# Retention inside the input product of the second mixer, head by head, with the sample states in 32 pieces

## The chip, the cores and the metric

The kernel runs on one core of a Trainium2 chip. The metric is the device time of one execution in microseconds (us); a kernel's time is the median of its runs. Of the core's engines, PE (TensorE) multiplies and transposes, DVE (VectorE) and ACT (ScalarE) do elementwise work, POOL (GpSimd) and SP (SyncE) mostly start DMA transfers. Each engine works through its own instructions in the written order, and semaphores hold one engine until another has got far enough.

## The reference

One step of a decoder with two layers for a prompt of 256 tokens and 8 samples of 4 tokens each (T = 288 token columns in all), everything in float32. A layer is a mixer, a cross-attention to 256 memory tokens and a convolutional FFN, each between norms. Layer 1's mixer is the retention that is changed here:

```python
z = h @ w_in_odd[o]                       # 1024 x 6144
q, k, v, g = jnp.split(z, [nq, 2 * nq, 2 * nq + nv], axis=-1)   # 4 heads: q, k 256 wide, v, g 512 wide
q = rope(q...) * (RET_DK ** -0.5); k = rope(k...)
r, s_new = retention(q, k, v, s_prev, log_g)   # prompt: two chunks of 128; samples: one chunk of 4 each
r = (r - mean(r)) * rsqrt(var(r) + EPS)        # per head and token
out = (silu(g) * r) @ w_out_odd[o]             # 2048 x 1024

# one chunk of retention, per head h, gamma = exp(log_g[h]):
scores = (q @ k.T) * dmat
o = scores @ v + (q @ s_prev) * q_decay
s_new = gamma ** L * s_prev + (k * k_decay).T @ v
```

The samples bring `state_retention`, 8 x 4 matrices of 256 x 512, and return as many: 16.8 MB in and 16.8 MB out. The prompt starts from zero and returns four such matrices.

## The kernel before, in words

**A weight product.** `Gemm` describes a product; all of them share one pipeline. A chunk is 1024 rows of 256 weight columns (1 MB). SP loads it into one of four slots of `raw` (L286). ACT rounds it to `wh` (L324), DVE takes the rest `wl = raw - wh` (L327), both in two buffers. PE then runs two tiles of 128 output columns per chunk, each of 24 matmuls over T columns: `wh*hh + wh*hl + wl*hh` for 8 row blocks (L392, helper `products`). A buffer of `wh` comes free when PE is through with both tiles of its chunk (`w_used`), and a slot of `raw` when `wl` is made (`lo_ready`).

**The second mixer** (`pe_odd`, `act_odd`, `dve_odd`, `pool_retention`) has two stages. First the input product, 24 chunks and 48 tiles in the order of the weight's columns: all q and k (DVE turns them by the rope, L876 to L880), all v, all g. Behind some of its chunks PE turns values and keys into token rows. Then the retention of all heads in 8 units, `UNITS` = (head, chunk of the prompt). Unit n also handles sample n, for all four heads: 8 matmuls of 512 columns read its old states (L1194, four heads at once in the four column groups of the array, into one bank), 8 matmuls give its new key-value products (L1207, two banks in turn), and after each of these DVE updates a quarter state in place (L946, `update`). PE's order in a unit is written out by hand: scores, old states, products, chunk state (L1229), output (L1236, L1241), products, transposes of the normed rows (L556).

**The states** stand in the four slots of `raw`, two samples at a time, 1 MB each half. SP starts their loads (`load_states`, L303) after the weight chunks of the product; from the third sample on a load waits until POOL's store of the slot (L584) has landed. The weights of the output product `w_out_odd` come behind them in SP's queue (L284 waits for the last two stores).

**The output product** (L392 again) starts when DVE has written the low part of the gated samples (L1005).

Of the kernel before, what the change touches and what calls it, by code (L numbers as in the profile page):

```python
# [15 lines left out]
F32 = mybir.dt.float32  # L16
# [5 lines left out]
P = 128  # L22
# [41 lines left out]
def build(nc, a, outs):  # L64
# [31 lines left out]
    with ctx:  # L96
# [92 lines left out]
        gs = ExitStack()  # L189
        gS = sb("gS", [16, T], F32, gs)  # L190
        gs.close()
        h2l = sb("h2l", [8, T], F32R, od)
        h2h = sb("h2h", [8, T], F32R, od)
        V4 = sb("V4", [RH * RDV], F32R, od)
        vR = sb("vR", [2, RH * RDV], F32, od)
        kR = sb("kR", [2, RH * RDK], F32, od)
        cR = sb("cR", [8 * P + 4], F32, od)
        cS = sb("cS", [12 * NS + 8], F32, od)

        QM = sb("QM", [8, DEC_B * (NS + DEC_T)], F32, od)  # L200
        K4 = sb("K4", [RH * RDK], F32, od)
        gp = ExitStack()
        cs = sb("cs", [2, T], F32, gp)
        cr = sb("cr", [2, T], F32, gp)
        rA = sb("rA", [2, T], F32, gp)
        rB = sb("rB", [2, T], F32, gp)
        vt = sb("vt", [4, T], F32, gp)
        vhS = sb("vhS", [4, NS], F32R, gp)
        v4T = sb("v4T", [4, 4, NS], F32, gp)
        gp.close()  # L210
        K4m = sb("K4m", [2, RH * RDK], F32R, od)
        ks = ExitStack()
        k4T = sb("k4T", [8, 4, NS], F32, ks)
        kd = sb("kd", [8, NS], F32, ks)
        kdh = sb("kdh", [8, NS], F32R, ks)
        ks.close()
        S1 = sb("S1", [2, RDV], F32, od)
        S2 = sb("S2", [2, RDV], F32, od)
        scr = sb("scr", [2, P], F32, od)
        qd = sb("qd", [2, P], F32, od)  # L220
        rn = sb("rn", [RDV], F32, od)
        rg = sb("rg", [4, P], F32, od)
        od.close()
        scS = rowsn[:].rearrange("p (h i) -> p h i", h=RH)

        def state_slot(b, hp):


            return (G["out", 1].first + 2 + 2 * (b % 2) + hp) % 4

        def state(b, h):
            return raw[:, state_slot(b, h // 2), 4 * (h % 2):4 * (h % 2) + 4, :].rearrange("p (d x) n -> p d (x n)", d=2)

        def states_dram(x, b, hp):
            return x[0, b, 2 * hp:2 * hp + 2].rearrange("h (d p) e -> p (h d) e", p=P)

        def states(b, hp):
            return raw[:, state_slot(b, hp)].rearrange("p (k x) n -> p k (x n)", k=4)
# [23 lines left out]
        def load_weights(e, g):  # L262
            w = g.w

            def step(i):
# [5 lines left out]
                for idx in range(g.per):  # L271
# [15 lines left out]
            if g.steps > 2:  # L287
# [5 lines left out]

        def load_states(e):

            for b in range(DEC_B):
                for hp in range(2):
                    if b < 2:

                        e.wait_ge(lo_ready, CREDIT + G["out", 1].first - 2 + 2 * b + hp + 1)  # L300
                    else:
                        e.wait_ge(s(f"SR_out{b % 2 * 2 + hp}"), 16 * (b // 2))
                    e.dma_start(states(b, hp), states_dram(a["state_retention"], b, hp)).then_inc(s(f"SR_in{b % 2 * 2 + hp}"), 16)  # L303
# [55 lines left out]
        def products(pe, g, pairs, freed, base, natural=False, i0=0, i1=None, turn=0,  # L359
                     hook=None, need=None):  # L360
# [5 lines left out]
            def step(i):  # L366
                for idx in range(g.per):
# [4 lines left out]
                    for j in range(2):  # L372
                        t = 2 * half + j
                        if kc == 0:
                            pe.wait_ge(freed, i * 4 + base + t - 3)
                        for n_k in range(kn):
# [182 lines left out]
        KR_BANKS = (5, 6, 7, 6)  # L559
# [8 lines left out]
        qdecS = cS[:, 4 * NS:8 * NS].rearrange("p (h o i) -> p h o i", h=RH, o=1)  # L568
        kdecS = cS[:, 8 * NS:12 * NS].rearrange("p (h o i) -> p h o i", h=RH, o=1)
        maskS = lambda b: cS[:, 12 * NS + b:12 * NS + b + 1]  # L570
        gam = [float(np.float32(1) - np.float32(2.0) ** np.float32(-5 - h)) for h in range(RH)]
        UNITS = [(h, c) for h in range(RH) for c in range(2)]

        def pool_retention(pool, store):
# [5 lines left out]

            for n, (hp, c) in enumerate(UNITS):
                for half in range(2):
                    pool.wait_ge(s("SR_new"), 8 * n + 4 * half + 4)
                    pool.dma_start(states_dram(ret_sample, n, half), states(n, half)).then_inc(s(f"SR_out{n % 2 * 2 + half}"), 16)  # L584
                    if c == 1 and half == 0:
                        pool.wait_ge(s("S2_ready"), 2 * hp + 2)
                        pool.dma_start(ret_prompt[0, 0, hp].rearrange("(t p) e -> p t e", p=P), S2[:]).then_inc(s("S2_stored"), 16)
# [1327 lines left out]
```

## Time and profile before

| | |
|---|---|
| median of 3 runs | 1323.36 us (1316.52 to 1324.07) |
| the profiled execution | 1325.95 us, span 1324.2 us |
| PE / PEld busy | 1193.6 us (90%) / 1094.7 us (83%) |
| DVE / ACT / POOL busy | 766.3 / 584.3 / 296.3 us |
| input product of layer 1 | from 544.4 to 718.8 us of the span |
| retention | from 718.8 to 841.8 us |
| HBM | 207.50 MB read, 25.16 MB written |

All times of rows are us from the span's start. PE is the busiest engine, but its busy time counts a matmul from its issue to a modelled end, so that neighbours overlap; what counts is the distance between starts, the gaps that the view of waits names, and the granted clock (1.00 is 2.4 GHz, 0.50 is 1.2 GHz).

### The profile page before, as it was taken

How to read it: one execution, taken by the hardware profiler on the slowest of the kernel's cores; microseconds unless marked ns; L12 is line 12 of the kernel's file. 1: busy time of each engine (PE TensorE's matmuls, PEld its weight loads, DVE VectorE, ACT ScalarE, POOL GpSimd, SP SyncE). 2: the span in 40 equal slices, each digit the busy share in tenths (PEclk: the TensorE clock that was granted, in tenths of full speed). 3: DMA queues.
4: the chain of work that ended last, by engine and by line, in shares of the span. 5: the costliest groups of instructions: out<-in, count | busy, mean ns of one | idle time of the engine just before them, and what ended most of it. 6: DMA issues, size and time to landing. Idle time of an engine off the chain costs nothing. (4 is left out here: it accounts for less than half of the span.)

```text
span 1324.2 us, 22941 instructions
## 1 busy us (share of the span) xinstructions
PE 1193.6 (90%) x8557; PEld 1094.7 (83%) x8557; DVE 766.3 (58%) x1020; ACT 584.3 (44%) x940; POOL 296.3 (22%) x521
## 2 busy tenths in 40 slices
PE   6999998897999999699999667899999779999995
PEld 4999897677999999699997323699986679999994
DVE  3585735317888833766555655447445167888433
ACT  5456543335666544423345211255434156566442
POOL 4001201114555520200000111003001135465302
PEclk9999999988999999799999888899999789999998
DMA  9647566632554356344444987747747334444431
GB/s 215 232 133 257 176 200 196 236 121 68 178 169 160 112 165 205 102 159 159 138 149 150 339 299 260 254 152 262 245 144 247 139 103 152 160 163 144 149 126 36
DMA packets 177267, 233.64 MB, mean 176 GB/s; under 512 B 5374, under 2 KB 153226, under 8 KB 177200
## 3 DMA queue, kind: packets, MB, share of 16 engines
q1 hardware_dynamic: 159088, 169.09, 39.3%
q0 software_dynamic: 18112, 63.60, 13.8%
q8 instruction: 48, 0.79, 0.3%
q14 instruction: 19, 0.16, 0.0%
HBM read 207.50 MB, written 25.16 MB: 176 GB/s over the span
## 5 line engine op out<-in xcount | busy, mean ns | idle before, releaser
L392 PE MATMUL ps<-hh,wh 128*128 128x288 f32 x1600 | 487.2, 304 | 34.7 <-DVE hl L450 28.2
L327 DVE TENSOR_TENSOR wl<-raw,wh 128x2048 fp32r<-128x2048 f32 (+2 forms) x154 | 331.7, 2154 | 314.4 <-ACT wh L324 314.4
L392 PE MATMUL ps<-hl,wh 128*128 128x288 f32 x1600 | 480.0, 300 | 0.0
L392 PE MATMUL ps<-hh,wl 128*128 128x288 f32 x1600 | 478.2, 299 | 0.0
L324 ACT ACTIVATE wh<-raw 128x2048 fp32r<-128x2048 f32 (+3 forms) x154 | 277.7, 1803 | 296.6 <-PE ps L392 283.5
L392 PEld LDWEIGHTS ps<-hh,wh 128*128 128x128 f32 x1600 | 307.2, 192 | 41.5 <-issue 33.7
L392 PEld LDWEIGHTS ps<-hh,wl 128*128 128x128 f32 x1600 | 309.0, 193 | 0.0
L392 PEld LDWEIGHTS ps<-hl,wh 128*128 128x128 f32 x1600 | 308.3, 193 | 0.3
L392 PE MATMUL ps<-aH,wh 128*128 128x288 f32 x352 | 104.2, 296 | 0.0
L392 PE MATMUL ps<-aL,wh 128*128 128x288 f32 x352 | 103.8, 295 | 0.0
L392 PE MATMUL ps<-aH,wl 128*128 128x288 f32 x352 | 103.6, 294 | 0.0
L458 POOL TENSOR_TENSOR mT<-mT,rstd 128x288 f32<-128x288 f32 x42 | 40.8, 1005 | 228.0 <-DVE rstd L433 228.0
L392 PE MATMUL ps<-wh,mh 128*128 128x256 f32 x256 | 75.1, 293 | 4.8 <-DVE wl L327 4.8
L584 POOL DMA_DIRECT2D out<-raw x16 | 12.2, 761 | 275.8 <-DVE raw L946 275.8
L392 PE MATMUL ps<-wh,ml 128*128 128x256 f32 x256 | 73.8, 288 | 0.0
L392 PE MATMUL ps<-wl,mh 128*128 128x256 f32 x256 | 73.7, 288 | 0.0
L1466 POOL TENSOR_TENSOR aL<-pd,aH 128x288 f32 (+1 forms) x44 | 68.6, 1578 | 4.2 <-ACT aH L1592 4.2
L392 PEld LDWEIGHTS ps<-aH,wl 128*128 128x128 f32 x352 | 66.3, 188 | 0.0
L392 PEld LDWEIGHTS ps<-aL,wh 128*128 128x128 f32 x352 | 66.1, 188 | 0.0
L392 PEld LDWEIGHTS ps<-aH,wh 128*128 128x128 f32 x352 | 66.0, 187 | 0.0
L946 DVE SCALAR_TENSOR_TENSOR raw<-raw,ps 128x512 f32<-128x512 f32 x64 | 41.5, 680 | 41.1 <-PE ps L1207 40.8
L1718 DVE SCALAR_TENSOR_TENSOR cb<-zb,cwT,cb 128x288 f32<-128x288 f32 x88 | 59.3, 712 | 0.8 <-ACT cb L1602 0.4
(286 smaller groups left out, 1649.4 us busy)
## 6 DMA issues: line engine op xcount, KB each, us to landing
raw<-w_ffn_up SPq DMA_DIRECT2D x44, 1024.0 KB, 5.1
raw<-w_in_odd SPq DMA_DIRECT2D x24, 1024.0 KB, 5.2
ring<-cache_mem_k POOLq DMA_DIRECT2D x16, 1024.0 KB, 5.6
ring<-cache_mem_v POOLq DMA_DIRECT2D x16, 1024.0 KB, 5.7
raw<-state_retention SPq DMA_DIRECT2D x16, 1024.0 KB, 7.3
out<-raw POOLq DMA_DIRECT2D x16, 1024.0 KB, 6.2
raw<-w_ffn_down SPq DMA_DIRECT2D x16, 768.0 KB, 4.5
raw<-w_in_even SPq DMA_DIRECT2D x10, 1024.0 KB, 6.7
```

The source lines that it names most:

```text
L324: e.activation(wh[:, c % 2, 0:kn, :], src, ACT.Copy).then_inc(hi_ready, 1)
L327: e.tensor_tensor(wl[:, c % 2, 0:kn, :], src, wh[:, c % 2, 0:kn, :].bitcast(F32), ALU.subtract).then_inc(lo_ready, 1)
L392: mm = pe.matmul(out, lhsT, rhs, start=(kc == 0 and n_k == 0 and n == 0), stop=(kc == g.nk - 1 and n_k == kn - 1 and n == 2))
L458: pool.tensor_tensor(mT[:, t, :], mT[:, t, :], rstd[:], ALU.mult).then_inc(scaled, 1)
L584: pool.dma_start(states_dram(ret_sample, n, half), states(n, half)).then_inc(s(f"SR_out{n % 2 * 2 + half}"), 16)
L946: dve.scalar_tensor_tensor(out=st, in0=st, scalar=gL(k // 2, DEC_T), in1=ps[:, 2 + k % 2, :], op0=ALU.mult, op1=ALU.add).then_inc(s("SR_ne ...
L1466: pool.tensor_tensor(aL[:, i * 2 + j, :], pd[:, j, :], aH[:, i * 2 + j, :].bitcast(F32), ALU.subtract).then_inc(s("a_lo"), 1)
L1718: dve.scalar_tensor_tensor(out=groups(cb[:, t, :]), in0=zb[:, t, :, 1:5], scalar=ftap(l, 1, tile), in1=groups(cb[:, t, :]), op0=ALU.mult, ...
```

## The change

The columns of the input product are taken head by head (`odd_cols`): for each head q, k, v, 8 tiles each, and then all gates in 16 tiles. With W = n // 8 the window of tile n, windows 0 to 3 are the heads, and 4 and 5 the gates. All retention work stands between the matmuls of these tiles. `amid(n)` runs after 12 of the 24 matmuls of tile n, `behind(n)` after the last one; both belong to the head of the window before (transposes of values, chunk states, outputs, transposes of normed rows) or to the own one (scores, keys).

The sample states become 32 pieces U = 8*head + sample of 512 KB, one behind each of the tiles 10 to 41. They have four buffers of their own (`st`) and no longer use `raw`. POOL starts their loads as well as their stores; piece U+3 is loaded when the store of piece U-1 has landed. The 8 matmuls on an old state are now four column blocks of 128 of one head in the four column groups. The result has token rows of four blocks in it, and four more matmuls per head (`select`) bring them to the layout for the norm, where before one norm did all heads at once.

On PE a unit before read, from the old states of a sample (L1194) to the scores of the next unit:

```order
L1194 MATMUL ps<-raw,QM 32x512 x8
L1207 MATMUL ps<-V,K4m 128x512 x2
L1229 MATMUL ps<-vR,kR 128x512 x2
L1207 MATMUL ps<-V,K4m 128x512 x2
L1236 MATMUL ps<-vR,scr 128x512
L1207 MATMUL ps<-V,K4m 128x512 x4
L556 MATMUL ps<-ident,rn 128x128 x4
L1218 MATMUL ps<-mT,sq 128x128 x2
```

The change has, from the last matmul of tile 20 to the first of tile 21 (st: a state's buffer, rn: normed rows):

```order
L1358 MATMUL ps<-hh,wl 128x288
L550 MATMUL ps<-ident,rn 128x32 [waits ro_rn]
L550 MATMUL ps<-ident,rn 128x32 x3
L1269 MATMUL ps<-st,QM 32x128 [waits SR_in2]
L1269 MATMUL ps<-st,QM 32x128 x7
L1278 MATMUL ps<-V,K4m 128x512 [waits SR_new,K4m_ready]
L1278 MATMUL ps<-V,K4m 128x512 [waits SR_new]
L1358 MATMUL ps<-hh,wh 128x288 [waits oz]
```

A tile now carries one piece with two products, where a unit carried eight in a row; the matmuls on the old states have a quarter of the columns and are four times as many.

On DVE a unit before had eight updates (L946) among the other steps of the unit:

```order
L968 TENSOR_TENSOR scr<-cR,ps 128x128
L970 TENSOR_TENSOR qd<-mT,cR 128x256
L955 TENSOR_TENSOR rg<-gS,ps 128x512
L946 SCALAR_TENSOR_TENSOR raw<-raw,ps 128x512 x2
L963 TENSOR_TENSOR hl<-rg,hh 128x4x128
L946 SCALAR_TENSOR_TENSOR raw<-raw,ps 128x512 x2
L985 SCALAR_TENSOR_TENSOR S<-S,ps 128x512 x2
L946 SCALAR_TENSOR_TENSOR raw<-raw,ps 128x512
L1012 BN_STATS small<-ps 128x6
```

In the change tile 11, in window 1, reads (rr, L917, L918: the rope; L979 to L987: the norm of prompt rows; L940, L941: the first steps of the samples' own keys):

```order
L979 BN_STATS small<-ps 128x6
L980 BN_AGGR small<-small 128x2
L913 TENSOR_TENSOR rr<-ps,cr 128x576
L917 TENSOR_TENSOR mT<-rr 128x288
L918 TENSOR_TENSOR mT<-rr 128x288
L986 RECIPROCAL small<-small 128x1
L987 TENSOR_SCALAR rn<-ps,small 128x512
L964 SCALAR_TENSOR_TENSOR st<-st,ps 128x512 x2
L940 COPY kdup<-mT 128x128
L941 TENSOR_TENSOR kd<-mT,cS 128x64
```

The two updates of the tile's piece stand behind the evacuation of the tile itself; behind the rest of the keys follows the split of a weight chunk (L319).

POOL's own queue before held only stores in this stage; now loads and stores alternate:

```order
L587 DMA out<-st 128x2x512 x2
L580 DMA st<-state_retention 128x2x512
L587 DMA out<-st 128x2x512
L580 DMA st<-state_retention 128x2x512
L587 DMA out<-st 128x2x512
L590 DMA out<-S 128x2x512
```

A load stands behind the store of the piece before it, and, through its wait, behind the landing of a store that was started one piece earlier. The core of the diff:

```diff
+    def odd_cols(i, half):
+        if i >= 2 * RH:
+            return 2 * RH * RDK + RH * RDV + 2 * CW * (i - 2 * RH) + CW * half
+        if i % 2:
+            return 2 * RH * RDK + RDV * (i // 2) + CW * half
+        return RH * RDK * half + RDK * (i // 2)
...
-            G["in", l] = gemm("in_odd", a["w_in_odd"][l // 2])
+            G["in", l] = gemm("in_odd", a["w_in_odd"][l // 2], (8,), odd_cols)
...
+        st = sb("st", [4, 2, RDV], F32, od)
...
-                    if g is G["out", 1] and (i, idx) in ((0, 2), (1, 0)):
-                        if i == 0:
-                            load_states(e)
-                        for slot in (2 * i, 2 * i + 1):
-                            e.wait_ge(s(f"SR_out{slot}"), 16 * (DEC_B // 2))
...
+            for U in range(4):
+                load(U)
+            for U in range(RH * DEC_B):
+                h, b = divmod(U, DEC_B)
+                pool.wait_ge(s("SR_new"), 2 * U + 2)
+                pool.dma_start(state_dram(ret_sample, U), st[:, U % 4]).then_inc(s(f"SR_out{U % 4}"), 16)
...
+                if U >= 1 and U + 3 < RH * DEC_B:
+                    pool.wait_ge(s(f"SR_out{(U - 1) % 4}"), 16 * ((U - 1) // 4 + 1))
+                    load(U + 3)
...
+            def update(U):
+                h, b = divmod(U, DEC_B)
+                for dt in range(2):
+                    dve.wait_ge(s("SU_ps"), 2 * U + dt + 1)
+                    x = st[:, U % 4, dt, :]
+                    dve.scalar_tensor_tensor(out=x, in0=x, scalar=gL(h, DEC_T), in1=ps[:, OS + dt, :],
+                                             op0=ALU.mult, op1=ALU.add).then_inc(s("SR_new"), 1)
...
+                if n == 0:
+                    for p in range(2):
+                        after(dve.memset(QM[p][:], 0.0))
...
+            def sample_state(U):
+                h, b = divmod(U, DEC_B)
+                pe.wait_ge(s(f"SR_in{U % 4}"), 16 * (U // 4) + 16)
+                if b == 0:
+                    pe.wait_ge(s("QM_ready"), h + 1)
+                for dt in range(2):
+                    for j in range(4):
+                        mm = pe.matmul(ps[j * NS:(j + 1) * NS, OR, 0:P], QM[h % 2][:, dt, b * NS:(b + 1) * NS],
+                                       st[:, U % 4, dt, j * P:(j + 1) * P], start=False, stop=b == DEC_B - 1 and dt == 1,
+                                       skip_group_check=True, tile_position=(0, j * NS))
...
+                for dt in range(2):
+                    if U:
+                        pe.wait_ge(s("SR_new"), 2 * U - 1 + dt)
+                    pe.matmul(ps[:, OS + dt, :], K4m[:, U % 2, dt * P:(dt + 1) * P], V4[h % 2][:],
+                              start=True, stop=True).then_inc(s("SU_ps"), 1)
+
+            def select(h):
+                pe.wait_ge(s("rows_out"), h + 1)
...
+                for j in range(4):
+                    mm = pe.matmul(ps[0:NS, OC, j * P:(j + 1) * P], ident[:, j * NS:(j + 1) * NS], rowsC[:], start=True, stop=True)
+                mm.then_inc(s("sel_ps"), 1)
...
+            for n in range(TILES):
+                c = g.first + n // 2
+                bank, j = tile_bank(n), n % 2
+                if j == 0:
+                    pe.wait_ge(lo_ready, c + 1 + CREDIT)
...
+                for k in range(DT):
+                    if n == 0:
+                        pe.wait_ge(h_lo, DT * q + k + 1)
+                    w_h, w_l = wh[:, c % 2, k, j * P:(j + 1) * P], wl[:, c % 2, k, j * P:(j + 1) * P]
+                    for x, (lhsT, rhs) in enumerate(((w_h, hh[:, k, :]), (w_h, hl[:, k, :]), (w_l, hh[:, k, :]))):
+                        mm = pe.matmul(ps[:, bank, 0:T], lhsT, rhs, start=k == 0 and x == 0, stop=k == DT - 1 and x == 2)
+                    if k == 3:
+                        amid(n)
+                mm.then_inc(w_used, 1)
+                if n == 1:
+                    ssq(pe, 2 * q)
+                behind(n)
...
-                             need=lambda k: pe.wait_ge(s("rg_lo"), 9 + k // 8))
+                             need=lambda k: pe.wait_ge(s("g_lo"), k // 2 + 1),
+                             enter=lambda t: pe.wait_ge(s("oz"), TILES - 3 + t))
```

The gates (silu), the product with them and the high and low parts of the result run in windows 4 and 5, and only the last eighth of them after the last tile; the output product starts with the heads that are ready.

## Rows read from the trace of the kernel before

**Rows 1.** Busy time by stretch: span, then each engine's busy us, granted clock, DMA.

```profile
544.40:718.80 174.40, 170.42 (x1243) 166.59 (x1244) 103.54 (x156) 66.13 (x89) 0.91 (x2) 0.97 0.45 148
718.80:841.80 123.00, 83.87 (x333) 37.60 (x333) 77.09 (x141) 24.02 (x35) 15.01 (x20) 0.84 0.82 287
```

**Rows 2.** PE's waits from 718.8 to 842: us in total, times, longest.

```profile
PE ps L1194 <- DMA raw<-state_retention: 19.1, 3, 6.8
PE ps L1207 <- DVE raw L946: 11.6, 17, 0.9
PE ps L556 <- DVE rn L1023: 6.3, 9, 2.9
PE ps L392 <- DVE hl L1005: 1.8, 1, 1.8
```

**Rows 3.** Stretches in which PE worked at the low clock, by the same view.

```profile
731.70:735.10 3.40, 3.40 (x18) 0.60 (x16) 1.40 (x4) 1.67 (x2) 0.76 (x1) 0.50 0.48 177
762.26:765.80 3.54, 3.54 (x16) 0.66 (x16) 0.00 (x0) 0.00 (x0) 0.00 (x0) 0.50 0.89 299
791.92:796.50 4.58, 4.58 (x18) 1.49 (x19) 0.18 (x1) 0.00 (x0) 0.00 (x0) 0.50 0.73 285
822.21:827.30 5.09, 5.09 (x19) 1.81 (x20) 0.69 (x2) 0.00 (x0) 0.00 (x0) 0.50 0.37 135
841.80:847.70 5.90, 5.90 (x25) 5.90 (x25) 0.19 (x1) 0.00 (x0) 0.71 (x1) 0.50 0.78 263
```

**Rows 4.** PE in order of time, one unit and the end before it: start, us, instruction, idle.

```profile
802.55 0.50 PE L1207 MATMUL ps<-V,K4m 128*128 128x512 f32 x1 [0.62 <-DVE raw L946]
803.94 0.50 PE L1207 MATMUL ps<-V,K4m 128*128 128x512 f32 x1 [0.90 <-DVE raw L946]
...
805.36 0.61 PE L1218 MATMUL ps<-mT,sq 128*128 128x128 f32 x4
805.90 1.92 PE L1194 MATMUL ps<-raw,QM 128*32 128x512 f32 x16
807.75 0.73 PE L1207 MATMUL ps<-V,K4m 128*128 128x512 f32 x2
...
812.61 0.49 PE L1207 MATMUL ps<-V,K4m 128*128 128x512 f32 x1 [0.30 <-DVE raw L946]
814.00 0.50 PE L1207 MATMUL ps<-V,K4m 128*128 128x512 f32 x1 [0.90 <-DVE raw L946]
814.92 0.66 PE L556 MATMUL ps<-ident,rn 128*128 128x128 f32 x4 [0.42 <-DVE rn L1023]
815.42 0.61 PE L1218 MATMUL ps<-mT,sq 128*128 128x128 f32 x4
```

**Rows 5.** PE in order of time: short matmuls, in the attention and in the product.

```profile
1008.64 1.09 PE L1279 MATMUL ps<-kTb,qB 128*32 128x256 f32 x16
1009.66 2.00 PE L556 MATMUL ps<-ident,ring 128*128 128x128 f32 x16
...
689.18 1.12 PE L1153 MATMUL ps<-mT,k4T 128*64 128x32 f32 x16
690.23 0.40 PE L392 MATMUL ps<-hh,wh 128*128 128x288 f32 x1
```

**Rows 6.** DVE and PE in order of time at the input product's start.

```profile
557.83 0.76 DVE L867 TENSOR_TENSOR cr<-cs,rstd 128x576 f32<-128x576 f32 x1
558.78 0.76 DVE L876 TENSOR_TENSOR rA<-ps,cr 128x576 f32<-128x576 f32 x1 [0.19 <-DVE cr L867]
...
561.09 2.28 DVE L327 TENSOR_TENSOR wl<-raw,wh 128x2048 fp32r<-128x2048 f32 x1
...
563.50 0.39 PE L392 MATMUL ps<-hh,wh 128*128 128x288 f32 x1 [1.84 <-DVE wl L327]
```

**Rows 7.** PE in order of time: 59 matmuls of the product lie between these starts.

```profile
570.85 0.29 PE L392 MATMUL ps<-hl,wh 128*128 128x288 f32 x1
...
578.71 0.30 PE L392 MATMUL ps<-hh,wh 128*128 128x288 f32 x1
```

**Rows 8.** DVE's groups from 540 to 847: busy us, mean ns, idle before.

```profile
L327 DVE TENSOR_TENSOR wl<-raw,wh 128x2048 fp32r<-128x2048 f32 x25 | 57.2, 2290 | 32.4 <-ACT wh L324 32.4
L946 DVE SCALAR_TENSOR_TENSOR raw<-raw,ps 128x512 f32<-128x512 f32 x64 | 41.5, 680 | 41.1 <-PE ps L1207 40.8
L919 DVE MEMSET QM<- 128x2304 f32 x1 | 2.0, 1978 | 0.4 <-issue 0.4
```

**Rows 9.** DMA issues from 718.8 to 842: KB each, median us to landing; POOL's issue time.

```profile
out<-raw POOLq DMA_DIRECT2D x16, 1024.0 KB, 6.2
raw<-state_retention SPq DMA_DIRECT2D x13, 1024.0 KB, 7.5
out<-S POOLq DMA_DIRECT2D x4, 512.0 KB, 5.6
...
L584 POOL DMA_DIRECT2D out<-raw x16 | 12.2, 761 | 275.8 <-DVE raw L946 275.8
```

More of the change, by code:

```diff
@@ L292, in load_weights @@
                     step(i)
[L294 to L303, printed above, removed]
         def target(g, i, idx, last):
@@ L653, in act_odd @@
-            for i in range(4, 9):
-                for idx in range(2):
-                    if idx == 0 and i > 4:
-                        naturals(i - 1)
-                    if i == 8:
-                        gates(i, idx)
-                    split(act, *target(g, i, idx, False), True)
-            run(act, g, True, gates, 9, 10)
-            run(act, g, True, gates, 10, 11)
-            for r in range(2):
-                act.wait_ge(s("k4_ps"), r + 1)
-                act.activation(K4[:, 512 * r:512 * r + 512], ps[:, 5 + r, :], ACT.Copy).then_inc(s("K4_ready"), 1)
@@ new lines, in dve_odd @@
+            GATED = {6: (0, 1, 2), 7: (3, 4), 8: (5, 6), 9: (7, 8), 10: (9,), 12: (10, 11), 13: (12,), 14: (13,), 15: (14,)}
+            LOW = {8: 0, 9: 1, 10: 2, 11: 3}
+            for n in range(TILES):
+                W, u = divmod(n, 8)
+                h = W - 1
+                prompt = 1 <= W <= RH
+                own = W < RH
+                U = n - 10
+                i, r = divmod(n, 4)
+                if W >= 2 and u == 2:
+                    moments("S", W - 2, 0)
+                if W >= 2 and u == 3:
+                    scaled_rows("S", W - 2, 0)
+                if prompt and u in (3, 4):
+                    moments("P", h, u - 3)
+                if prompt and u in (6, 7):
+                    last_state(h, u - 6)
+                tiles_ready(dve, g, i, r // 2, r % 2)
+                if not own:
+                    e = n - 32
+                    if e >= 8:
+                        dve.wait_ge(s("gated"), e - 7)
+                    dve.tensor_tensor(gate(e), ps[:, tile_bank(n), 0:T], rstd[:], ALU.mult).then_inc(s("oz"), 1)
+                elif u < 4:
+                    turn(n, head(W, "qk"[u // 2]))
+                else:
+                    keep(n, W, u - 4)
+                if n == 0:
+                    for p in range(2):
+                        after(dve.memset(QM[p][:], 0.0))
+                if prompt and u in (3, 4):
+                    scaled_rows("P", h, u - 3)
+                if own and u == 5:
+                    scores(W)
+                if own and u == 6:
+                    sample_scores(W)
+                if 0 <= U < RH * DEC_B:
+                    update(U)
+                if own and u == 2:
+                    own_queries(W)
+                if own and u == 3:
+                    own_keys(W)
+                for e in GATED.get(n - 32, ()):
+                    gated(e)
+                if n - 32 in LOW:
+                    gated_low(LOW[n - 32])
+                if n == TILES - 1:
+                    for p in range(4, 7):
+                        gated_low(p)
+                    gated(15)
+                if n % 2:
+                    split(dve, *target(g, i, r // 2, i == g.steps - 1), False)
@@ new lines, in scores @@
+            def scores(h):
+                if h == 0:
+                    pe.wait_ge(root_ready, 2 * q + 1)
+                elif h == 1:
+                    pe.wait_ge(s("V4_ready"), 1)
+                else:
+                    pe.wait_ge(s("rS_out"), h - 1)
+                pe.wait_ge(s("turned"), 4 * h + 4)
+                for c in range(2):
+                    tok = slice(c * CHUNK, (c + 1) * CHUNK)
+                    for dt in range(2):
+                        mm = pe.matmul(ps[:, OC, c * P:(c + 1) * P], head(h, "k")[:, dt, tok], head(h, "q")[:, dt, tok],
+                                       start=dt == 0, stop=dt == 1)
+                mm.then_inc(s("rs_ps"), 1)
```

733 lines of the change are left out of this document (365 added, 368 removed).

## The prediction

> **What bounds the kernel now.** I read busy time by stretch first. The input product of layer 1 takes 174.4 us, the retention behind it 123.0 [rows 1]. In the product the granted clock is 0.97 and PE hardly waits: PE bounds it, DVE is busy 103.5 us and the DMA engines 0.45 of the time. In the retention no engine is full: PE's issued work is 83.9 us by that view, the clock 0.84, the DMA engines 0.82. PE's waits name what is late: 19.1 us for states that have not landed, 11.6 for DVE's updates, 6.3 for the normed rows, 1.8 for the last gated samples, together 38.8 us [rows 2]. After each long wait PE works on at the low clock for 3.4 to 5.9 us, 22.5 us in five stretches [rows 3]; the same work would take half of that at the high clock, so 11.25 us are lost there. The last of these stretches is the start of the output product, which inherits the cold clock. So 38.8 + 11.3 = **50.1 us** between 718.8 and 847.7 are waiting or its after-effect. The rest is work that PE has to do anyway.
>
> **What the change gives back.** PE's retention work moves between matmuls that never run out, 48 tiles of 24 x 0.133 = 3.2 us each (7.86 us for 59 starts [rows 7]). If these cover every wait, the 50.1 us go. I checked the cover by the longest chains:
>
> - States. A buffer's turn is the store of 512 KB, 5.6 us, a load, at most the 7.5 us of the 1 MB load, two issues of 0.76 us [rows 9], and some 3 us from PE's read to the end of the update: 17.6 us for four pieces, 4.4 us each. A tile with a piece takes PE about 6.5 us (3.2 for the tile, 1.5 for the piece, the rest its share of a head's work). POOL starts the load of piece U+3 three tiles ahead, some 18 us. By volume, 32 such tiles are 208 us, in which 33.6 MB of states and 16 chunks of weights (16.8 MB) move: 242 GB/s, under the 287 that the retention reaches now.
> - Updates. A piece has two products and two updates of 0.68 us [rows 8] per tile, and the next products come a tile later. Before, the seventh and eighth product of a unit waited 0.30 and 0.90 us, in other units 0.6 and 0.9, because each of the two banks had to be read before its next product [rows 4].
> - DVE as a whole. Per window of 8 tiles it has 16 updates (10.9 us), 4 splits of 2.29 (9.2 us) and, at the lengths of its rows now, some 17 us of ropes, values and norms: 37 us in about 52 of PE's. ACT has less (90 us in both stages where DVE has 181 [rows 1]). A split of a chunk has two tiles of time, about 13 us, and it stands behind at most 6 us of other work on DVE's queue.
> - POOL's queue takes the loads from SP. With the stores they are 64 issues of at most 0.76 us, 49 us in over 200; what queues behind a waiting load is only the next store, and its buffer is needed three tiles later.
> - The end. Only the gates of the last tile and a quarter of the gated rows come behind it; 2 tiles of the output product (6.4 us) need none of them, so their cover is there.
>
> **What it costs PE.** Matmuls that only change place cost nothing. New are:
>
> - The old states: 256 matmuls of two passes each, 512 passes of 128 columns in place of 128 of 512. The trace has no such shape. In a unit 16 passes take 805.90 to 807.75, 1.85 us or 0.116 each, 14.8 us in all [rows 4]. The attention has 16 passes of 256 columns in column groups: 1.02 us, 0.064 each; and 16 passes with only 32 columns, without groups, still take 1.05 us, 0.066 each [rows 5]. So halving the columns from 512 nearly halved the time, but below 256 the price seems to be one of the pass. I take 0.064: 32.8 us, **18.0 more**. Lower bound: a quarter of 0.116, nothing more than now.
> - `select`: 16 matmuls of 128 columns. The scores, two such matmuls, take 0.54 us [rows 4]: 16 x 0.27 = 4.3 us. At 0.064 per pass it would be 2.0.
> - The products within the samples are 32 passes instead of 8: 24 x 0.064 = 1.5 us at most. The sample rows are transposed in 16 pieces instead of 4: 12 x 0.125 = 1.5 us (4 in 0.50 [rows 4]).
> - The start. There DVE is late already: PE waits for the split that starts at 561.09 [rows 6]. The change puts two memsets into this chain, each a quarter of the 1.98 us [rows 8] and a semaphore round of some 0.1 to 0.2 [rows 6], 1.2 us together; nothing covers them.
>
> In all 18.0 + 4.3 + 1.5 + 1.5 + 1.2 = **26.5 us**. Switching between product and retention costs something too, but there are about as many such places before (some 56 in the units and 14 in the product) as now (about 75), so I count none. I leave 2 us for single waits at window borders. The sum: 50.1 - 26.5 - 2 = **21.6 us less**. Against the profiled execution's 1325.95 that is 1304.4; the median of the runs is 2.6 us lower, and against it the forecast is 1323.4 - 21.6, **about 1302 us**.
>
> **One rule weighed.** The price of the old states rests on 0.064 us per pass. The Trainium skill ("TensorE: Matmul & The Clock Gate", Measured speedup vs the span model) says that matmuls in different column groups start some 4 ns apart and run side by side. By that, a group of four passes of 128 columns would cost little more than one pass, and the 512 passes no more than the 14.8 us that they cost now. The measured 0.064 at 256 columns agrees with that rule, the 0.066 at 32 columns speaks for a floor per pass that it does not name.
>
> **The rivals.**
>
> - Short passes are cheap (18%): the pass price scales with the columns, as from 512 to 256. Then the 18.0 us are not spent: 1302 - 18 = 1284. For it is the pair 0.116 and 0.064, against it the 0.066 of L1153, which however has no column groups.
> - The cover leaks a little (17%): a tile with a piece loses 0.3 us on average, in queues that run in order on three engines; 32 x 0.3 = 9.6 us: 1312. The single waits of 0.3 us before [rows 4] show how easily this comes.
> - The updates still hold PE (12%), on the other side: behind each tile the two products wait for DVE as the last two of a unit did, 0.6 + 0.9 us, because DVE first has evacuation, norms and keys of that tile in its queue. 32 x 1.5 = 48 us: 1302 + 48 = 1350, slower than before. It decides from 21.6 / 32 = 0.68 us per tile on. Against it: the products need the update of the tile before, a tile of 6.5 us away, and DVE is busy only some 70%.
> - The ring of four states binds (5%): if both transfers took twice their time now, a turn would be 30.7 us, 7.7 per piece, 1.2 us more than a tile; 38 us: 1340. The Trainium skill ("DMA: Bandwidth & Descriptors", Bandwidth) warns of transfers under 1 MiB, since each has a fixed part. The trace agrees, 5.6 us for 512 KB beside 6.2 for 1 MB [rows 9], and with four in turn it is latency that a tile's time hides.
> - That nothing changes is excluded: the order of instructions is another one, and the waits of [rows 2] have other partners.
>
> **Numbers.** The forecast has 48%, with its own range of 1292 to 1312. From 1280 to 1322 lie it, most of the cheap passes and the leak: about 82%. What can be told from no change is about 1%, 13 us. Faster than 1310: the forecast, the cheap passes and a third of the leak, 0.70; within 1%: 0.17, mostly the leak; slower: 0.13, of the last two rivals without their mild forms.
>
> **What would show it.** After the change the distance from the product's first matmul to the output product's first should be about 275 us, with the clock at 1.00 from some 25 us on and no low stretch at the output product. The old states' 16 passes should stand 1.0 us ahead of the products; 0.5 would be the cheap rival. PE's waits for `st` updates and for states should be under 5 us in all; a wait for the updates behind most tiles is the slow rival, a wait for `state_retention` the ring. The first wait for `wl` should be about 3 us. What would prove the whole wrong is a tile time well over 6.5 us with PE waiting inside the tiles, for normed rows or ACT's copies.

## The result and the profile after

The changed kernel takes 1277.69 us (median of 4 runs, 1276.65 to 1278.11); the kernel before took 1323.71 beside it. The ratio is 0.9663, 95% interval 0.9633 to 0.9692. Forecast were 1302 us with a range of 1280 to 1322: the direction was right, but 46 us came where 21.6 were expected, and the time lies 2.3 us below the range.

The profiled executions, 1325.95 and 1277.42 us, are 48.5 us apart. From the input product's first matmul to the output product's first, "the stage" from here on, were 300.6 us (541.19 to 841.80) and are 253.74 (541.74 to 795.48): 46.9 us of it are here. The prediction had named about 275 us for the stage and 6.5 us for a tile with a piece; 31 of these tiles take 5.9 us on average (591.86 to 773.41, from the first piece to the last).

Busy time by stretch, before, the whole stage and then its first 59 us (columns as in [rows 1]):

```profile
541.19:841.80 300.61, 256.43 (x1580) 205.63 (x1581) 183.84 (x301) 91.43 (x126) 19.13 (x26) 0.91 0.60 203
541.20:560.00 18.80, 17.70 (x93) 16.23 (x94) 14.18 (x19) 6.64 (x12) 4.11 (x6) 0.74 0.33 111
560.00:600.00 40.00, 38.16 (x275) 37.93 (x274) 27.94 (x34) 11.51 (x6) 0.00 (x0) 0.96 0.48 156
```

The same view after, the whole stage, its first stretches, two from inside, and the output product's start:

```profile
541.74:795.48 253.74, 249.68 (x2032) 214.85 (x2033) 185.90 (x327) 98.14 (x144) 53.10 (x74) 0.99 0.73 241
541.74:560.00 18.26, 17.15 (x99) 15.69 (x100) 14.80 (x20) 6.62 (x12) 7.02 (x10) 0.82 0.70 229
560.00:600.00 40.00, 37.04 (x293) 34.06 (x292) 28.49 (x53) 14.89 (x16) 0.72 (x1) 1.00 0.43 144
640.00:680.00 40.00, 40.00 (x346) 34.01 (x337) 29.04 (x59) 12.83 (x19) 10.74 (x15) 1.00 0.80 268
795.48:802.00 6.52, 6.52 (x50) 6.33 (x48) 5.51 (x8) 4.55 (x6) 0.00 (x0) 1.00 0.40 136
```

PE is busy all of 640 to 680, the clock is 1.00 from 560 to the stage's end, and the output product starts warm, where [rows 3] had 5.90 us at 0.50. DVE's work is the same (183.84 and 185.90 us) in 47 us less. The DMA share rises from 0.60 to 0.73 over the stage; the 0.82 of the retention alone [rows 1] is spread out.

PE's waits after, 541 to 796, all of them, beside [rows 2]:

```profile
PE ps L1358 <- DVE hl L444: 8.1, 3, 7.0
PE ps L1358 <- DVE wl L319: 3.0, 1, 3.0
```

The first stands in both kernels (8.1 us before too) and belongs to the norm ahead of the product. Nothing waits for states, updates or normed rows: 38.8 us are gone to the last tenth. One more wait of before is gone: 1.6 us in the input product, ahead of the stretch of [rows 2], in which transposes of values waited for ACT's copies:

```profile
PE ps L556 <- ACT V L652: 1.6, 4, 0.4
```

The wait for `wl` at the start is 2.96 us, where 1.84 [rows 6] and 1.2 more were expected.

PE in order of time, a tile's middle with work of the head (columns as in [rows 4]):

```profile
642.86 0.59 PE L1200 MATMUL ps<-vR,scr 128*128 128x512 f32 x1
642.88 0.69 PE L1358 MATMUL ps<-hh,wh 128*128 128x288 f32 x1
643.41 0.29 PE L1358 MATMUL ps<-hl,wh 128*128 128x288 f32 x1
...
644.73 0.29 PE L1358 MATMUL ps<-hh,wl 128*128 128x288 f32 x1
644.96 0.65 PE L1269 MATMUL ps<-st,QM 128*32 128x128 f32 x16
645.53 0.73 PE L1278 MATMUL ps<-V,K4m 128*128 128x512 f32 x2
646.10 0.29 PE L1358 MATMUL ps<-hh,wh 128*128 128x288 f32 x1
```

A piece is seen whole: 0.57 us for 16 passes on the old state (644.96 to 645.53), where 1.0 was forecast and 0.5 named for the cheap rival, and 0.57 for the two products (645.53 to 646.10). Behind them the tile goes on without a gap.

DVE's groups after, 541 to 796, beside [rows 8]; then the DMA issues, 560 to 790, beside [rows 9]:

```profile
L319 DVE TENSOR_TENSOR wl<-raw,wh 128x2048 fp32r<-128x2048 f32 x24 | 54.9, 2286 | 6.2 <-ACT wh L316 6.2
L964 DVE SCALAR_TENSOR_TENSOR st<-st,ps 128x512 f32<-128x512 f32 x64 | 41.0, 683 | 9.7 <-PE ps L1278 9.7
```

```profile
raw<-w_in_odd SPq DMA_DIRECT2D x18, 1024.0 KB, 7.4
out<-st POOLq DMA_DIRECT2D x32, 512.0 KB, 4.3
st<-state_retention POOLq DMA_DIRECT2D x28, 512.0 KB, 5.9
```

One operation takes DVE what it took before. Its idle time before updates has fallen from 41.1 us to 9.7.

### The profile page after: what moved, and what is told of

Same layout as the page of the kernel before. It is cut to its first block and busy times, and to the rows that moved or that the text cites. A ratio compares the mean times of both kernels' runs of the same rounds, so it can differ in the third digit from the quotient of the medians.

```text
span 1275.7 us, 23764 instructions
## 1 busy us (share of the span) xinstructions
PE 1183.2 (93%) x9009; PEld 1099.7 (86%) x9009; DVE 774.2 (61%) x1054; ACT 596.9 (47%) x965; POOL 330.7 (26%) x569
## 3 DMA queue, kind: packets, MB, share of 16 engines
q0 software_dynamic: 22976, 80.38, 18.8%
## 5 line engine op out<-in xcount | busy, mean ns | idle before, releaser
L319 DVE TENSOR_TENSOR wl<-raw,wh 128x2048 fp32r<-128x2048 f32 (+2 forms) x154 | 331.6, 2153 | 278.6 <-ACT wh L316 278.5
L386 PE MATMUL ps<-hh,wh 128*128 128x288 f32 x1216 | 368.5, 303 | 22.5 <-DVE hl L444 20.1
L1358 PE MATMUL ps<-hh,wh 128*128 128x288 f32 x384 | 124.6, 324 | 11.1 <-DVE hl L444 8.1
L587 POOL DMA_DIRECT2D out<-st x32 | 23.0, 718 | 180.6 <-DVE st L964 176.1
```

The costliest lines, as they stand in the source:

```text
L319: e.tensor_tensor(wl[:, c % 2, 0:kn, :], src, wh[:, c % 2, 0:kn, :].bitcast(F32), ALU.subtract).then_inc(lo_ready, 1)
L386: mm = pe.matmul(out, lhsT, rhs, start=(kc == 0 and n_k == 0 and n == 0), stop=(kc == g.nk - 1 and n_k == kn - 1 and n == 2))
L587: pool.dma_start(state_dram(ret_sample, U), st[:, U % 4]).then_inc(s(f"SR_out{U % 4}"), 16)
L1358: mm = pe.matmul(ps[:, bank, 0:T], lhsT, rhs, start=k == 0 and x == 0, stop=k == DT - 1 and x == 2)
```

## The experiments

Distances are from one matmul's start to the next one's, added up by line over the stage. Differences of times are between medians, against the changed kernel's 1277.7 or, where the kernel before is edited, its own median in that job; each ratio is against the kernel before on the same chip.

**The pass price, doubled (x1).**

```diff
-                for dt in range(2):
+                for dt in (0, 0, 1, 1):
```

> The changed kernel with every pass on the old states issued twice (1024 passes of 128 columns in place of 512, 32 per piece; the samples' share from the old states is so counted twice). Theory: the forecast missed mainly because a pass in the four column groups costs 0.036 us here and not 0.064, and all of it lies on PE's path: 512 more passes, 18.4 us more, about 1296. Rival A, the price taken in the prediction: 512 x 0.064 = 33 us more, 1310. Rival B, the passes run in a cover (beside the loads of weights or behind a wait that ends later anyway): under 5 us more.

1294.27 us, ratio 0.9786 (0.9724 to 0.9849): 16.6 more. PE in order of time, one piece:

```profile
643.45 1.08 PE L1269 MATMUL ps<-st,QM 128*32 128x128 f32 x32
644.46 0.72 PE L1278 MATMUL ps<-V,K4m 128*128 128x512 f32 x2
```

1.01 us for 32 passes, 0.57 for 16. The old states' distances go from 18.37 us to 32.34, 13.97 more, and the stage from 253.74 to 267.63, 13.9 more. So all of it lies on PE's path; an added pass costs 0.027 us. Near the theory, far from the 33 us of the prediction's price. What is left of the 0.57 us, 0.57 - 16 x 0.027 = 0.14, comes once per piece and not with the passes.

The changed kernel has a row for the same pass without neighbours: the matmuls of `select` have the same shape, but all stand in one column group:

```profile
635.48 0.29 PE L1358 MATMUL ps<-hh,wl 128*128 128x288 f32 x1
635.71 1.06 PE L1289 MATMUL ps<-rowsC,ident 128*32 128x128 f32 x8
636.70 1.12 PE L1193 MATMUL ps<-vR,kR 128*128 128x512 f32 x2
```

Inside the eight, from the third on, each starts 0.109 us behind the one before; in four groups side by side a pass costs a quarter of that, 0.027.

**Fewer column groups (x4).**

```diff
-                    for j in range(4):
-                        mm = pe.matmul(ps[j * NS:(j + 1) * NS, OR, 0:P], QM..., st[:, U % 4, dt, j * P:(j + 1) * P], ...)
+                    for j in range(2):
+                        mm = pe.matmul(ps[j * NS:(j + 1) * NS, OR, 0:2 * P], QM..., st[:, U % 4, dt, 2 * j * P:2 * (j + 1) * P], ...)
```

> The changed kernel with the old states read in two column groups of 256 columns in place of four of 128 (256 passes in place of 512, and two selections per head in place of four). Theory, the price of a group goes by columns streamed and groups side by side: 16 passes of 0.036 become 8 of 0.1 or so (512 columns on end in each of two groups, 2 x 256 x 0.42 ns x 4 for float32 = 0.85 us per piece, in place of 0.57): 32 x 0.28 = 9 us more, and about 1 less for the selections. Rival, each pass has a floor that the columns below 256 do not lower (the price that the prediction took): 256 passes fewer x 0.03 to 0.064, 8 to 16 us less.

1295.72 us, ratio 0.9798 (0.9735 to 0.9860): 18.0 more. PE in order of time, one piece:

```profile
647.19 1.06 PE L1269 MATMUL ps<-st,QM 128*32 128x256 f32 x8
648.18 0.73 PE L1278 MATMUL ps<-V,K4m 128*128 128x512 f32 x2
```

Half as many passes, twice as wide, take 0.99 us instead of 0.57. The stage grew by 16.6 us, 13.2 of them at the old states; 0.8 are the products within the samples, and most of the rest is a longer low clock at the stage's start. The selections did not get cheaper (3.96 and 3.91 us). The direction is the theory's, the size (9) was too small. A floor of 0.064 us for a pass of 128 columns is refuted by x1 and x4; shorter passes side by side were not run.

**Updates on the way again (x2).**

```diff
-                    if U:
-                        pe.wait_ge(s("SR_new"), 2 * U - 1 + dt)
-                    pe.matmul(ps[:, OS + dt, :], ...
+                    if U or dt:
+                        pe.wait_ge(s("SR_new"), 2 * U + dt)
+                    pe.matmul(ps[:, OS, :], ...
```

> The changed kernel with both new key-value products of a piece in one bank, so that the second of them waits for the update of the first, 32 times, as the products of a unit waited for updates before. Theory: an update on the way costs PE the whole distance between starts, about 1.4 us as in the unit before (802.55 to 803.94) in place of 0.28, while the view of waits shows only 0.6 to 0.9 of it, since it counts from the modelled end of the product: 32 x 1.1 = 36 us more at the most, 25 to 36, and the view of waits shows 19 to 29, at least a fifth less than the time. Rival: the view of waits shows all that is lost, and the time rises by what it shows, within 2 us.

1323.9 us, ratio 1.0004 (0.9979 to 1.0029): the whole gain is gone. PE's waits in the stage, and one piece on PE in order of time:

```profile
PE ps L1278 <- DVE st L964: 31.4, 32, 2.2
```

```profile
644.11 0.64 PE L1269 MATMUL ps<-st,QM 128*32 128x128 f32 x16
644.69 0.50 PE L1278 MATMUL ps<-V,K4m 128*128 128x512 f32 x1
645.97 0.49 PE L1278 MATMUL ps<-V,K4m 128*128 128x512 f32 x1 [0.78 <-DVE st L964]
```

The view shows 31.4 us. The products' distances grew from 18.17 to 58.19, 40.0 more: a product that is followed at once costs 0.28 us, but in front of a wait its whole 0.50 us counts as busy. The remaining 5.8 of the stage's 45.8 us are about half of the 13.1 us for which the clock was low beyond the 6.7 without the edit; 6.8 us of these lie behind waits for updates (662.8 and 731.1), the rest at the stage's start, ahead of the first piece, and so hardly belong to the edit. The theory's direction is seen, time lost beyond what the view shows, but both sizes lie above its ranges: 1.25 us per wait by the distances where 1.1 was the most, 31.4 us in the view where 29 was.

**No pieces at all (x3).** `sample_state`, `update`, `own_keys` and the loads and stores of states are not called.

> The changed kernel without the 32 pieces: no loads and stores of sample states (33.6 MB), no matmuls on old states, no new key-value products, no updates and no keys for them; the samples' new states and their share from the old ones are left out. Theory: PE bounds the stage, and the pieces cost just the distance between their starts, 18.4 (old states) + 18.2 (products) = 36.6 us, and some 4 us of switching: 35 to 41 us less, 1237 to 1243. Rival: contention of DMA or DVE still holds PE, then more goes, 45 us and over. Second rival: weights or DVE's splits bound the stage, then PE's saving turns into waits for wl, under 25 us.

1242.16 us, ratio 0.9389 (0.9328 to 0.9450): 35.5 less; the stage is 216.23 us, 37.5 less, against 36.5 for the distances of the pieces' matmuls. Busy time of the whole stage:

```profile
542.07:758.30 216.23, 212.17 (x1456) 190.45 (x1457) 146.01 (x263) 85.44 (x112) 7.01 (x10) 0.98 0.39 128
```

With the DMA share down from 0.73 to 0.39 and 40 us of DVE's work gone, the stage gets shorter by just what PE no longer does. Neither transfers nor DVE held the changed kernel.

**The kernel before, its waits taken away one after the other (x5, x6, x11).** x5 leaves the stores out:

```diff
-                        for slot in (2 * i, 2 * i + 1):
-                            e.wait_ge(s(f"SR_out{slot}"), 16 * (DEC_B // 2))
+                        e.wait_ge(s("SR_new"), 56 + 8 * i)
...
-                    pool.dma_start(states_dram(ret_sample, n, half), states(n, half)).then_inc(...)
```

> The kernel before without its 16 stores of the sample states (that output is left out); the loads of states and of the output product's weights wait for the updates instead, so they start earlier. Theory: the states' wait was 19.1 us of PE's and the low clock behind it about half of the 11.25 us, so 19 to 26 us less, 1298 to 1304, with the wait for states gone from PE's view and the waits for updates still there. Rival: the updates take over (PE then stands longer at them), and less than 10 us go.

1304.22 us, ratio 0.9836 (0.9812 to 0.9861): 20.9 less, within the theory. The stage is 25.4 us shorter (300.61 to 275.25); about 3 of these are a shorter low clock at its start (7.0 us in place of 13.0), and 2.2 came back behind it. The wait for states is gone from PE's view; these two stayed as they were:

```profile
PE ps L1205 <- DVE raw L944: 11.6, 17, 0.9
...
PE ps L555 <- DVE rn L1021: 6.3, 9, 2.9
```

x6 makes the updates short:

```diff
-                st = state(b, k // 2)[:, k % 2, :]
-                dve.scalar_tensor_tensor(out=st, ..., in1=ps[:, 2 + k % 2, :],
+                st = state(b, k // 2)[:, k % 2, 0:32]
+                dve.scalar_tensor_tensor(out=st, ..., in1=ps[:, 2 + k % 2, 0:32],
```

> The kernel before with updates of 32 columns in place of 512 (only these columns of the sample states get their new value). Theory: PE lost about 25 us at the updates by the distance between starts and not the 11.6 that the view of waits names, so the start to start time of the 64 products falls from 43.4 us to about 20, and the kernel gets 18 to 25 us faster, unless the states' wait takes a part of it back. Rival: the view of waits is right, then at most 11.6 us go, and the start to start time falls by no more.

1320.98 us, ratio 0.9968 (0.9942 to 0.9994), 4.1 less: a miss. The products' distances fell from 43.42 to 39.25 only. The view's waits for updates fell by 8.4 us, but 6.8 came back at the states and the normed rows:

```profile
PE ps L1194 <- DMA raw<-state_retention: 23.4, 4, 8.3
PE ps L556 <- DVE rn L1023: 8.8, 9, 1.9
...
PE ps L1207 <- DVE raw L946: 3.2, 8, 0.4
```

DVE in order of time at a unit's end in x6 shows what is left of the chain:

```profile
781.72 0.19 DVE L946 SCALAR_TENSOR_TENSOR raw<-raw,ps 128x32 f32<-128x32 f32 x1 [0.98 <-PE ps L1207]
781.82 0.69 DVE L1012 BATCH_NORM_STATS2 small<-ps 128x6 f32<-128x512 f32 x1
782.55 0.18 DVE L1014 BATCH_NORM_AGGREGATE small<-small 128x2 f32<-128x6 f32 x1
782.65 0.15 DVE L946 SCALAR_TENSOR_TENSOR raw<-raw,ps 128x32 f32<-128x32 f32 x1
783.09 0.16 DVE L1019 RECIPROCAL small<-small 128x1 f32<-128x1 f32 x1 [0.29 <-ACT small L709]
783.29 0.81 DVE L1023 TENSOR_SCALAR rn<-ps,small 128x512 f32<-128x512 f32 x1
```

The update that the last product waits for stands behind the 0.87 us of the norm's moments. So the update's length is only a part of what holds PE there: the rest is what DVE's queue has ahead of it, and the transposes behind wait for the norm's whole chain anyway. How large PE's loss at the updates was, x6 left open.

x11 is x5 without any update and without the products' waits:

```diff
-                    if n >= 2:
-                        pe.wait_ge(s("SR_new"), n - 1)
```

> The kernel before without stores of the sample states (as x5) and without DVE's 64 updates too; PE's products wait for nothing any more, and loads wait only for PE's read (the new sample states are left out). Against x5 (1304.2). Theory: at the updates PE lost clearly more than the 11.6 us that the view of waits shows, some 18 to 20 by the distances between starts of all matmuls with 512 columns and the weights' (230.85 before, 211.78 after the change), and the normed rows, which stand behind updates on DVE's queue, come 2 to 4 us earlier: 20 to 24 us less than x5, 1280 to 1284. Rival: the view of waits is right, 11.6 and at most 4 of the rows, 12 to 16 us less, 1288 to 1292.

1288.84 us, ratio 0.9739 (0.9704 to 0.9774): 15.4 less than x5 (13.7 if each is taken from the kernel before in its own job, 34.6 and 20.9), on the rival's side. Of PE's waits one is left in the retention that counts:

```profile
PE ps L555 <- DVE rn L1014: 14.4, 9, 2.6
```

The products wait for nothing, and the rows' wait rose from 6.3 to 14.4. The stage lost 11.7 us (275.25 to 263.52). With the 8.1 that came back as waits for rows 19.8 us were freed, but 4.2 of that are clock (low for 22.7 and 14.4 us in the stage): some 15.6 us at the updates against the 11.6 of the view. The difference is about what x2 shows beyond the view, (40.0 - 31.4) / 32 = 0.27 us per wait, for 17 waits. The theory that 18 to 20 were lost there falls.

**Two state buffers (x10).** `U % 4` becomes `U % 2`, and:

```diff
-                if U >= 1 and U + 3 < RH * DEC_B:
+                if U >= 1 and U + 1 < RH * DEC_B:
...
-                    load(U + 3)
+                    load(U + 1)
```

> The changed kernel with two state buffers in place of four: the load of piece U+1 waits for the store of piece U-1. Theory (the prediction's ring rival, with after's durations): a turn is store 4.3, load 6.1, two issues 1.5 and 2.5 to 3 from PE's read to the update's end, 14.5 us for two pieces or 7.2 a piece, while a tile with a piece takes 253.7 / 48 to 5.9 us: 32 x 1.3 to 1.9 = 42 to 61 us more, and the low clock on top; waits for state_retention on PE. Rival: loads and stores of other buffers overlap so that the turn is hidden: under 10 us more.

1394.24 us, ratio 1.0532 (1.0498 to 1.0566), 116.6 more. PE's wait in the stage, and POOL's queue in order of time:

```profile
PE ps L1269 <- DMA st<-state_retention: 77.9, 29, 5.4
```

```profile
652.97 0.71 POOL L587 DMA_DIRECT2D out<-st  x1 [8.01 <-DVE st L964]
653.67 0.74 POOL L580 DMA_DIRECT2D st<-state_retention  x1
661.45 0.71 POOL L587 DMA_DIRECT2D out<-st  x1 [7.04 <-DVE st L964]
662.15 0.74 POOL L580 DMA_DIRECT2D st<-state_retention  x1
```

The mechanism is the ring rival's, the size twice the theory's. A piece takes 8.4 to 11.6 us instead of 7.2, because the load of piece U+1 stands on POOL's queue behind the wait for the updates of piece U, so nothing overlaps; and the clock is low for 88.9 us of the stage. With four buffers the same order does no harm (no wait for states in the changed kernel): the load that waits there is three pieces ahead.

**Improvements tried (x7, x8, x9).** x7 moves the work from a tile's middle to its end:

```diff
-                    if k == 3:
+                    if k == DT - 1:
```

> The changed kernel with the work that stands in the middle of a tile moved to the tile's end, ahead of what stands there already, so there are some 30 switches fewer between the product's matmuls and the others. Theory: each switch costs PE some 0.1 us between starts (a product's matmul behind another kind has 0.2 to 0.55 us in place of 0.133), 3 to 5 us less in all, 1273 to 1275. Rival: the work in the middle gave DVE and ACT their lead, then the waits of PE for them rise by more, and the time is longer by 5 us or more.

1279.10 us, ratio 0.9647 (0.9629 to 0.9664): a miss, no gain, the stage even 1.8 us longer. The weights' distances fell by 9.7 us, but those of all other matmuls rose by 11.5. The lines at 642.86 above show it: the last matmul of the other kind has 0.02 us to the next start and the first of the tile 0.53 behind it, together 0.55, about what the two take apart (0.43 and 0.13). Switching was counted at the wrong place: between matmuls on the whole array it hardly costs anything. Of matmuls on a part of the array (stationary operands of 32 or 64 columns or rows) x7 says nothing, since PE goes 38 times from the whole array to a part and back in it, as often as in the changed kernel.

x8 and x9 (x9 contains x8):

```diff
+                else:
+                    dve.wait_ge(s("ret_in"), 48)
+                    for p in range(2):
+                        dve.memset(QM[p][:], 0.0).then_inc(s("QM_zero"), 1)
...
-                act.activation(rowsC[:], ps[:, OR, 0:P], ACT.Copy).then_inc(s("rows_out"), 1)
+                for j in range(4):
+                    ins = act.activation(rn[0:NS, 2, j * P:(j + 1) * P], ps[j * NS:(j + 1) * NS, OR, 0:P], ACT.Copy)
+                ins.then_inc(s("rows_out"), 1)
...
-                if W >= 2 and u == 2:
-                    select(W - 2)
```

> The changed kernel with the two memsets of QM moved ahead of the first norm's reciprocal, and the split of the third weight chunk put between the first tile's evacuation and its rope. Theory: PE's only long wait inside the product, 3.0 us for wl, falls to 0.9, 2 us less, 1275 to 1276. Rival: DVE is then late for the rope or the second split, and the wait only moves: no change.

1277.34 us, ratio 0.9635 (0.9619 to 0.9651). The wait for `wl` is gone and the stage is 251.39 us, 2.35 shorter, as forecast, but the time, for which 2 us less were forecast, is the same. What was gained is lost behind the stage. After, and then x8, in the same stretches of the following stages:

```profile
800.00:900.00 100.00, 97.00 (x750) 95.37 (x749) 57.97 (x51) 52.70 (x79) 13.14 (x14) 1.00 0.66 221
900.00:1000.00 100.00, 86.07 (x716) 70.57 (x716) 37.09 (x61) 31.92 (x56) 14.80 (x20) 0.93 0.58 203
```

```profile
800.00:900.00 100.00, 97.61 (x748) 96.56 (x748) 57.00 (x50) 52.52 (x78) 13.14 (x14) 0.98 0.65 221
900.00:1000.00 100.00, 86.87 (x708) 70.90 (x707) 35.92 (x60) 31.90 (x56) 14.77 (x20) 0.91 0.59 204
```

The granted clock is lower there, 0.98 for 1.00 and 0.91 for 0.93, though the work is the same.

> The changed kernel with the early zeros of x8 and without `select`: ACT copies the four row blocks of a head's old-state result straight to the place where the norm stands (four copies of 32 rows in place of one of 128), and DVE takes moments and norm from there. Theory: PE bounds the stage, so the 32 selecting matmuls give back their distance between starts, 3.96 us, and the early zeros the 2.35 us that they gave between the stage's ends; 6 us less in the stage (247 to 248), 1271 to 1273 in all, unless the clock of the later stages takes 2 us of it as it did in x8. Rival: ACT's three more copies per head or DVE's norm come late, and PE waits for the samples' rows: no gain, with a wait for rn or R in PE's view.

1273.28 us, ratio 0.9609 (0.9583 to 0.9635): 4.4 us less than the change, the fastest version. The stage is 247.75 us, 6.0 shorter, as forecast; the stages behind took some 2 back.

## Why the prediction missed

The parts of the sum beside the distances of the two profiled executions, in us. Forecast are the prediction's terms; its 8.3 us for the four low-clock stretches of the retention are put where most of the work in them is. A wait counts with the matmul ahead of it: so 3.4 of the 6.3 us of waits for normed rows stand with the products, and 2.9 with the transposes.

| part | forecast | before | after | measured |
|---|---|---|---|---|
| scores, with the wait for states ahead of the old states | -19.1 | 23.80 | 3.76 | -20.0 |
| weights' and key-value products, chunk states, outputs (updates, most waits for rows, start) | -14.4 | 230.85 | 211.78 | -19.1 |
| old states | +10.9 | 21.61 | 18.37 | -3.2 |
| transposes, with the last rows and last gates | -3.8 | 20.57 | 11.35 | -9.2 |
| `select`, within samples, samples' scores | +5.8 | 2.04 | 6.76 | +4.7 |
| single waits | +2.0 | | | 0 |
| ahead of the stage and behind it | -3.0 | | | -1.7 |
| sum | -21.6 | | | -48.5 |

- **The step that failed** is "I take 0.064: 32.8 us, 18.0 more". The passes cost 0.036 on average and 18.37 us in all, 3.6 more than the 14.8 of before at the high clock (the fixed 0.14 comes 32 times and not 8, 24 x 0.14 = 3.4); 14.4 of the 26.9 us missing are this term. Its two good rows were 0.116 at 512 columns [rows 4] and 0.064 at 256 [rows 5]; the line through them gives 0.038 at 128. The choice went against it because of the 0.066 at 32 columns, a row of matmuls without column groups, whose passes follow one another. x1 and x4 show the price: 0.14 per piece, and for 16 passes 0.43 in four groups of 128 and about 0.85 for 8 in two groups of 256. That is work divided by the number of groups that run beside one another.
- **The rule weighed.** The Trainium skill ("TensorE: Matmul & The Clock Gate", Measured speedup vs the span model) says that matmuls in different column groups start some 4 ns apart and run side by side. The prediction set this rule aside for a floor that it does not name. It held: neighbours start 0.007 us apart in the trace, and four more passes, one in each group, cost 4 x 0.027 = 0.11 us together (x1), as much as one pass of `select` in a single group, 0.109. The 0.14 us that remain come with the change to a part of the array and back. The Trainium skill ("TensorEngine Tiling (Array Packing)", Key Properties) says that a change of the tiling mode drains the engine. The trace agrees: the product's last matmul has 0.23 us to the next start ahead of the passes and of `select`, and 0.13 ahead of matmuls on the whole array; `select`'s last has 0.20 where its others have 0.11; and the 0.14 did not double in x1. That it is a drain, and not something else that comes with the change, no run shows.
- **The cheap rival** (18%) was right in its mechanism, and with 1284 still 6 us too slow. The range's lower end was that case and 4 us; of the table's other parts all but the one ahead of the stage and behind it erred on the same side, and so the time fell out of the range.
- **What the change gives back** was right: all 38.8 us of waits went. x5 confirms some 21 for the states with their clock. x2 shows that a wait costs more than the view says, 40.0 for 31.4, and x11 puts the updates at some 15.6 for 11.6. For the 25 waits for updates and rows among the products, 0.27 us each beyond the view are, by estimate, 6.7 us that no term had.
- **The clock at the stage's start** was in no term. Before, the product ran at 0.74 up to 560 and at 0.96 up to 600, after at 0.82 and 1.00: by half of the low time, (0.26 x 18.8 + 0.04 x 40) - 0.18 x 18.3 = 3.2 us less. The same start varies between the experiments, so this is no merit of the change that the runs show.
- **Cover** held. The two leak rivals and the ring had no part: no wait behind the stage's first tiles. x3 shows that PE alone sets the stage, x10 that the ring would have been dear, and x2 that the slow rival's mechanism costs 46 us (some 3 of them the clock at the start) once the updates stand on the path; the two banks and the distance of a tile keep them off it.
- **Switching** at nothing was right only between matmuls on the whole array (x7). The count behind it set unlike things side by side, changes inside the units before and departures from the product after; from one line of PE's matmuls to another there were 90 changes in the stage and are 218. For matmuls on a part of it the starts in the trace show a price: 0.09 us ahead of them, 0.09 behind the last, and 0.10 more for the first matmul on the whole array behind them (a weights' matmul 0.24 there instead of 0.13). The stage has 38 such places after and had 10 before: 28 x 0.28 = 7.8 us, of which 3.4 are the fixed part of the passes above and some 4.4 stand in no term. The table's second row gave 4.7 more than forecast; the 6.7 of the waits and the 3.2 of the clock less these 4.4 are 5.5, so about 1 us stays open. That two things left out, the waits' rest and the changes to a part of the array, went against each other was luck.
- **The transposes** gave 5.4 us more than their term. 1.6 of it are the waits for ACT's copies, which lie ahead of the prediction's stretch; the rest stays open.
- **`select`** (forecast 4.3, measured 3.96) and the start (1.2 and 1.1) were right.

## What to carry to other kernels

Price a short matmul by rows of its own kind: passes in column groups by their columns divided by the groups that run side by side, with a fixed part for each change to a part of the array and back (0.28 us here), and not by the price of a short pass that runs alone. A wait that a view names also costs what the view still counts as busy ahead of it (0.27 us here) and the low clock behind it, so moving work between matmuls that never run out is worth more than the sum of the waits, as long as nothing on the way waits for another engine's answer (x2 lost all of it by one bank less). Where a queue alternates loads and stores that wait, count buffers by how many pieces ahead the load stands, not by the transfers' times.

## What was not expected of the hardware

The time behind the stage moves with the clock that is granted there, though the code is the same: over the profiles of the changed kernel, x8 and x1 it is 470.5, 472.9 and 473.3 us from the output product's start to PE's last matmul, and the low clock was granted for 30.7, 37.5 and 37.5 us of it. Half of the low time's difference is 3.4 us, which covers the 2.4 and 2.8. x7 lies on the other side, 468.8 us with 27.3 of low clock. A gain of 2 us in one stage can so vanish in the next, and is read from the stage, not from the sum.
